# Hybrid block on one core: four subtractions of the weight split move from GpSimd to VectorE

## The chip, the cores and the metric

The kernel runs on one core of one Trainium2 chip. The metric is the device time of one launch in microseconds; the figure for a kernel is the median of its runs.

## The reference

One transformer-like layer on 256 tokens of width 1024, all in fp32. Cut to what matters:

```python
h = h + hybrid_mixer(rms_norm(h, norm_mix), w_in, conv..., gates..., norm_lru_out, norm_attn_out, w_out)
h = h + memory_cross_attention(rms_norm(h, norm_cross), mem, norm_mem, w_xq, w_xkv, w_xo)
h = h + hier_moe(rms_norm(h, norm_ffn), router weights, w_gate_up, w_down)   # 32 experts, 2 per token
return rms_norm(h, norm_final)
```

The mixer projects the tokens to five parts of 512 columns (x_lru, g_lru, q, k, v). x_lru passes a short convolution and a gated linear recurrence and is multiplied by gelu(g_lru). q, k and v go through causal attention with 8 heads of 64. Both results are normalised and multiplied with w_out. The cross attention has 4 heads of 256 over 256 memory tokens. The mixture of experts holds 32 experts of two matrices, 6 MB each expert, all of which are read.

## The kernel before

**Two phases.** Phase A computes the mixer, the cross attention and the router, and ends at about 235 us. Phase B is a loop over eight batches of four experts, whose weights flow through a ring of on-chip units; its first loads are issued during phase A, each when the memory or the half that it needs has been used up.

**The dense weights** of phase A come as 30 halves of 128 x 2048 numbers, in the order of `STREAM` (line 57): halves 0 and 1 are x_lru, 2 and 3 q, 4 and 5 k, 6 and 7 v, 8 and 9 g_lru, 10 to 13 the memory keys (xk), 14 and 15 the first columns of w_out, and so on. TensorE multiplies in a rounded format (fp32r), so each half is split in two. ScalarE copies the raw half into the rounded high part (`split_hi`, the copy of line 899), and then another engine subtracts that from the raw half to get the low part (`split_lo`: `V.tensor_tensor(... subtract)`, line 1195, on VectorE, and line 1126 on GpSimd). TensorE forms three products for each chunk: activation low by weight high, activation high by weight low, and high by high (`channels`, line 561, and `tokens`, line 575). The activations are split likewise (line 1208).

**Buffers.** Raw halves land in four buffers (`landing`, m modulo 4). The load of half m is issued by SyncE once the low part of half m-4 is there (`await_split`). The two parts of a half lie in one of three slots (m modulo 3), so the high part of half m waits until TensorE has used half m-3.

**Who subtracts.** `POOL_LO = (6, 8, 10, 12)`: GpSimd makes the low parts of these four halves, VectorE those of the others. Each engine counts on its own semaphore (`w_lo`, `w_lo_pool`), and `await_split(eng, m)` waits for both counts. GpSimd also does the second part of half 0 (line 1134), powers of -0.5 for the norms (line 1120), three steps of gelu (lines 1143, 1145 and 1147) and sums of squares (lines 1157 and 1159).

**Order.** Every engine runs a list of work written out by hand, strictly in order. Around the change VectorE does: the low parts of the memory activations (`turned_lo("Tm")`, line 1208), half 7, the rotary embedding (lines 1290 to 1295), a step of the input gate (line 1300), half 9, two steps of the recurrence's input (lines 1304 and 1305), two copies of transposed q and k, half 11, the scan (line 1310), scores and maxima (lines 1315 to 1330), half 13, two normalisations of the softmax (line 1336), half 14, a copy, the end of gelu (lines 1346 and 1347), and the low part of the recurrence's result (`ylru_lo`, line 1352), for which TensorE waits ahead of half 14. TensorE does, from half 6 on: v (halves 6 and 7), transposes of q and k, g_lru (halves 8 and 9), scores (line 618), xk (halves 10 to 13), transposes of the softmax (lines 647 to 653), half 14 and the value products.

Of the kernel before, what the change touches and what calls it, by code (L numbers as in the profile page):

```python
# [17 lines left out]
F32 = mybir.dt.float32  # L18
F32R = mybir.dt.float32r
I32 = mybir.dt.int32  # L20
ALU = mybir.AluOpType
# [46 lines left out]
            "out1", "out5", "out3", "out7", None, "xv1", "xq0", "xq1", "xq2", "xq3", None, "xv3",  # L68
            None, "xo1", None, "xo3"]

POOL_LO = (6, 8, 10, 12)


PARAMS = {}
# [126 lines left out]
def block_kernel(nc, x, mem, dense, w_gate_up, w_down, norm_final, early, late, out):  # L201
    with ExitStack() as ctx:
# [3 lines left out]
        def sem(name):  # L206
            return ctx.enter_context(nc.semaphore(name))
# [42 lines left out]
        def const(name):  # L250
            a, n = CONSTS[name]
            return ctab[:, a:a + n]

        def param(name, c=None):
            a, n = PARAMS[name][0] + N_CONSTS, PARAMS[name][1]
            return ctab[:, a:a + n] if c is None else ctab[:, a + c:a + c + 1]
# [4 lines left out]
        def pb(job):  # L261
            return bank(BANK_OF[job])
# [41 lines left out]
        def pair(src, off, c):  # L304
            return tuple(src[:, off + HALF * part:off + HALF * part + HALF].rearrange("p (c t) -> p c t", c=c)
                         for part in range(2))

        def slot(m, c):
            return pair(split_w, UNIT * (m % SLOTS_W), c)
# [6 lines left out]
        def raw(m, c):  # L316

            return landing[:, HALF * (m % RAW):HALF * (m % RAW) + HALF].rearrange("p (c t) -> p c t", c=c)

        def chunks_of(m):  # L320
            return KC if STREAM[m // 2] in BY_COLUMNS else CT


        def rt(n, m=EXPERTS):
            return small[:, 256 + 64 * n:256 + 64 * n + NH * m].rearrange("p (h e) -> p h e", h=NH)
# [13 lines left out]
        freed = [sem(f"freed{b}") for b in range(BANKS)]  # L339
        raw_loaded = [sem(f"raw_loaded{r}") for r in range(RAW)]  # L340

        w_hi, w_lo, w_lo_pool = sem("w_hi"), sem("w_lo"), sem("w_lo_pool")
        w_lo_first = sem("w_lo_first")
        half_used = sem("half_used")
        x_loaded = [sem(f"x_loaded{h}") for h in range(NH)]
# [63 lines left out]
        def await_fill(eng, job):  # L409
            eng.wait_ge(filled[BANK_OF[job]], FILLS[job])  # L410

        def await_read(eng, job):
            eng.wait_ge(freed[BANK_OF[job]], FREED_AFTER[job])

        def await_first_read(eng, job):
            eng.wait_ge(freed[BANK_OF[job]], FREED_BEFORE[job] + 1)

        def await_split(eng, m):

            by_pool = sum(n in POOL_LO for n in range(m + 1))  # L420
            eng.wait_ge(w_lo, m + 1 - by_pool)
            if by_pool:
                eng.wait_ge(w_lo_pool, by_pool)

        def await_half_used(eng, m):
            if LAST_JOB[m]:
# [7 lines left out]
        def _(sp):  # L434
# [14 lines left out]
            def load_half(m):  # L449
                if m >= RAW:  # L450
                    await_split(sp, m - RAW)
                sp.dma_start(raw(m, chunks_of(m)), half_source(m)).then_inc(raw_loaded[m % RAW], 16)
# [20 lines left out]


            await_split(sp, HALVES - 4)
            load_expert(2, 2, 0, (0,))
            await_fill(sp, "xs3")
# [4 lines left out]
            await_fill(sp, "xv3")  # L482
            load_expert(1, 1, 1)
            await_split(sp, HALVES - 3)
            load_expert(2, 2, 0, (1,))
            await_fill(sp, "xpv3")
# [627 lines left out]
        @block.gpsimd  # L1114
        def _(pool):
            nc.gpsimd.memset(xlp[:, :, 0:CONV - 1], 0.0).then_inc(zeroed, 1)
            pool.wait_ge(early_loaded, 16)

            def power(col, n, done):
                nc.gpsimd.tensor_tensor(stat[:, RS + col:RS + col + n], stat[:, MS + col:MS + col + n],  # L1120
                                        const("power")[:, 0:n], ALU.pow).then_inc(done, 1)

            def split_lo(m):
                pool.wait_ge(w_hi, m + 1)
                hi, lo = slot(m, chunks_of(m))
                nc.gpsimd.tensor_tensor(lo, raw(m, chunks_of(m)), hi.bitcast(F32), ALU.subtract).then_inc(w_lo_pool, 1)

            for stage in (1, 2):
                pool.wait_ge(meansq, stage)
                power(2 * (stage - 1), 2, rstd)  # L1130
                if stage == 1:
                    pool.wait_ge(w_hi, 1)
                    hi, lo = slot(0, KC)
                    nc.gpsimd.tensor_tensor(lo[:, CT:], raw(0, KC)[:, CT:], hi[:, CT:].bitcast(F32), ALU.subtract
                                            ).then_inc(w_lo_first, 1)
            split_lo(6)
            split_lo(8)
            split_lo(10)

            pool.wait_ge(root_ready, 1)  # L1140
            for c in range(2):
                await_read(pool, f"gl{c}")
            nc.gpsimd.tensor_tensor(gate_r, gx, gx, ALU.mult).then_inc(pool_step, 1)
            pool.wait_ge(pool_step, 1)
            nc.gpsimd.tensor_scalar(gate_r, gate_r, GELU_CUBE, 1.0, ALU.mult, ALU.add).then_inc(pool_step, 1)
            pool.wait_ge(pool_step, 2)
            nc.gpsimd.tensor_tensor(gate_r, gate_r, gx, ALU.mult).then_inc(gelu_arg, 1)
            split_lo(12)

            for part in range(2):  # L1150
                if part:
                    for c in range(2):
                        await_first_read(pool, f"pv{c}")
                else:
                    pool.wait_ge(ylru_squared, 1)
                t = CT * part
                nc.gpsimd.tensor_tensor(sqT[:, t:t + 2], sqT[:, t:t + 2], sqT[:, t + 2:t + 4], ALU.add).then_inc(pool_step, 1)
                pool.wait_ge(pool_step, 3 + part)
                nc.gpsimd.tensor_tensor(sqT[:, t], sqT[:, t], sqT[:, t + 1], ALU.add).then_inc(squares_added, 1)
            await_read(pool, "ss")  # L1160
            power(SUB, 4, sub_rstd)
            for stage in (3, 4):
                pool.wait_ge(meansq, stage)
                power(2 * (stage - 1), 2, rstd)

            pool.wait_ge(rank_known, 1)
            over = rt(12)
            nc.gpsimd.tensor_scalar(over, rankm, float(SLOTS), None, ALU.is_ge).then_inc(over_ready, 1)
            for h in range(NH):
                pool.wait_ge(final_ms, h + 1)  # L1170
                power(FINAL + h, 1, final_rstd)

        @block.vector
        def _(dve):
# [3 lines left out]
            def link(ins):  # L1178

                steps[0] += 1  # L1180
                ins.then_inc(dve_step, 1)
                dve.wait_ge(dve_step, steps[0])

            def release(ins, job):
                ins.then_inc(freed[BANK_OF[job]], 1)
# [5 lines left out]
            def split_lo(m):  # L1191

                dve.wait_ge(w_hi, m + 1)
                hi, lo = slot(m, chunks_of(m))
                V.tensor_tensor(lo, raw(m, chunks_of(m)), hi.bitcast(F32), ALU.subtract).then_inc(w_lo, 1)  # L1195
# [10 lines left out]
            def rest(dst, src, gain, hi):  # L1206

                return V.scalar_tensor_tensor(dst, src, gain, hi.bitcast(F32), ALU.mult, ALU.subtract)  # L1208

            def turned_lo(prefix, dst, gain, cs=range(4)):  # L1210
                for c in cs:
                    await_first_read(dve, f"{prefix}{c}")
                    for k in range(2):
                        t = 2 * c + k
                        i = rest(dst[1][:, t], pb(f"{prefix}{c}")[:, 256 * k:256 * k + 256], param(gain, t), dst[0][:, t])
                    release(i, f"{prefix}{c}")

            def plain(job, dst, c=2):

                await_fill(dve, job)  # L1220
                src = pb(job).rearrange("p (c t) -> p c t", c=c) if c else pb(job)
                release(V.tensor_copy(dst, src), job)
# [5 lines left out]
            hi, lo = slot(0, KC)  # L1228
# [47 lines left out]
            i.then_inc(conv_done, 1)  # L1276
            split_lo(5)
            turned_lo("Tm", ms_, "norm_mem")
            split_lo(7)

            for name in ("q", "k"):
# [16 lines left out]
            for c in range(2):  # L1298
                await_read(dve, f"ig{c}")
            link(V.scalar_tensor_tensor(gate_i, gate_i, 1.0, xc, ALU.add, ALU.mult))  # L1300
            split_lo(9)
            dve.wait_ge(decay_ready, 1)
            dve.wait_ge(root_ready, 1)
# [1 line left out]
            link(V.tensor_tensor(root, root, gate_i, ALU.mult))  # L1305
            for c in (1, 3):
                plain(f"Tqk{c}", qkT[:, 2 * c:2 * c + 2])
            split_lo(11)
            for t in range(CT):
                i = V.tensor_tensor_scan(xc[:, t], decay[:, t], root[:, t], 0.0, ALU.mult, ALU.add)  # L1310
# [17 lines left out]
            for c in range(4):  # L1328
                await_read(dve, f"s1{c}")
            V.tensor_reduce(soft[:, 8:16], p1, AX.X, ALU.max, negate=True).then_inc(smax, 1)  # L1330
            split_lo(13)

            def normalize(h, p):
# [209 lines left out]
            with dve.Fori(0, BATCHES) as g:  # L1543
# [13 lines left out]
                for j in range(BATCH):  # L1557
                    n = BATCH * g + (j + 1)
# [18 lines left out]
            with dve.If(many > 0):  # L1577
# [13 lines left out]
                with dve.Fori(0, EXPERTS) as e:  # L1591
                    for h in range(NH):
                        n = NH * e + (h + 1)
# [13 lines left out]
            for h in range(NH):  # L1607
# [3 lines left out]
                for cb in range(2):  # L1611
                    n = slice(512 * cb, 512 * cb + 512)
# [21 lines left out]
```

## Time and profile before

| what | us |
|---|---|
| median of 3 runs | 672.67 (672.4 to 674.99) |
| the profiled execution, its own time | 671.75 |
| its span | 670.0 |
| TensorE matmul busy | 510.9 (76%) |
| VectorE busy | 220.9 (33%), 425 instructions |
| ScalarE busy | 168.9 (25%) |
| GpSimd busy | 41.0 (6%), 25 instructions |
| load of a dense half, issue to landing | 5.4 (median of 30) |
| HBM traffic | 237.85 MB, mean 355 GB/s |

A line number names the line of the program that issued an instruction, which may be a helper. Times of rows are counted from the start of the span.

### The profile page before, as it was taken

The page shows a single profiled execution, that of the slowest core. Times are in us where ns is not written, and L with a number is a line of the kernel's source. Part 1 is how long each engine was busy: PE and PEld are TensorE (multiplying, and loading weights), DVE is VectorE, ACT ScalarE, POOL GpSimd, SP SyncE. Part 2 cuts the span into 40 slices and gives each one's busy share as a digit, 9 for nine tenths or more (in the row PEclk, how much of TensorE's full clock was granted, in tenths as well). Part 3 has the DMA queues.
Part 4 walks back from the last instruction along what each step waited for, and adds up shares of the span by engine and source line. Part 5 has one row for each costly group of instructions (what it writes and reads, how often), then busy time and mean ns, then how long its engine had stood idle before and what let it go on. Part 6 is the DMA issues. An engine that isn't in the chain of part 4 may idle for free.

```text
span 670.0 us, 11410 instructions
## 1 busy us (share of the span) xinstructions
PE 510.9 (76%) x4768; PEld 351.9 (53%) x4768; DVE 220.9 (33%) x425; ACT 168.9 (25%) x325; POOL 41.0 (6%) x25
## 2 busy tenths in 40 slices
PE   3999999999999987978656756855684585657544
PEld 3988998789888654545223423422352252224221
DVE  3795987664653432212011200201120021012002
ACT  6558576363441211111010100101010001011002
POOL 2032441300000000000000000000000000000000
PEclk9999999999999799999867978978698898889889
DMA  8754733396579969999999999999999999999993
GB/s 345 285 194 183 314 127 142 138 398 248 186 282 382 357 238 425 425 430 427 427 426 427 422 425 426 429 427 426 427 426 424 423 429 427 427 426 427 423 425 156
DMA packets 25637, 237.85 MB, mean 355 GB/s; under 512 B 2832, under 2 KB 2960, under 8 KB 4368
## 3 DMA queue, kind: packets, MB, share of 16 engines
q1 hardware_dynamic: 25616, 237.55, 86.0%
q8 instruction: 15, 0.25, 0.1%
q14 instruction: 6, 0.05, 0.0%
HBM read 236.49 MB, written 1.05 MB: 355 GB/s over the span
## 4 chain that ended last, share of the span: by engine, by line
SPq 48%; PE 38%; DMA 7%; issue 3%; DVE 2%; ACT 1%; POOL 1%; DVEq 0%; POOLq 0%
SPq L447 30%; SPq L442 18%; PE psum L575 14%; PE psum L561 11%; DMA ring<-in_w_down 5%; PE psum L811 3%; PE psum L836 2%; DMA landing<-in_dense 1%; PE psum L794 1%; PE psum L544 1%; PE psum L709 1%; PE psum L732 1%; PE psum L845 1%; PE psum L758 1%; POOL stat L1120 1%
## 5 line engine op out<-in xcount | busy, mean ns | idle before, releaser
L811 PE MATMUL psum<-ring,xg 128*32 128x256 f32 x2048 | 152.6, 454 | 87.4 <-DMA ring<-in_w_gate_up 87.4
L811 PEld LDWEIGHTS psum<-ring,xg 128*32 128x32 f32 x2048 | 78.8, 126 | 154.6 <-issue 129.7
L575 PE MATMUL psum<-split_w,split_act 128*128 128x512 f32 x432 | 101.8, 393 | 1.2 <-DVE res L1379 1.2
L575 PEld LDWEIGHTS psum<-split_w,split_act 128*128 128x128 f32 x432 | 80.4, 188 | 18.3 <-DVE res L1379 1.7
L1562 DVE SCALAR_TENSOR_TENSOR small<-small,psum 128x128 f32<-128x128 f32 x32 | 9.2, 288 | 214.8 <-ACT small L1084 214.8
L1084 ACT ACTIVATE small<-psum 128x128 f32<-128x128 f32 x32 | 8.9, 277 | 279.3 <-PE psum L811 279.3
L836 PE MATMUL psum<-ring,small 128*32 128x256 f32 x1024 | 67.2, 400 | 12.9 <-ACT small L899 11.7
L561 PE MATMUL psum<-split_act,split_w 128*128 128x256 f32 x576 | 72.2, 289 | 0.9 <-DVE split_act L1208 0.9
L561 PEld LDWEIGHTS psum<-split_act,split_w 128*128 128x128 f32 x576 | 71.6, 197 | 1.7 <-DVE split_w L1229 1.2
L899 ACT ACTIVATE split_w<-landing 128x2048 fp32r<-128x2048 f32 x30 | 57.4, 1915 | 51.2 <-PE psum L575 27.6
L1195 DVE TENSOR_TENSOR split_w<-landing,split_w 128x2048 fp32r<-128x2048 f32 x25 | 58.9, 2361 | 30.6 <-ACT split_w L899 30.6
L1568 DVE COPY ybuf<-psum 32x256 f32<-32x256 f32 x64 | 27.2, 424 | 95.3 <-PE psum L836 94.8
L836 PEld LDWEIGHTS psum<-ring,small 128*32 128x32 f32 x1024 | 30.2, 113 | 40.0 <-ACT small L899 18.1
L899 ACT ACTIVATE ybuf<-psum 32x256 f32<-32x256 f32 x64 | 23.9, 373 | 72.5 <-PE psum L836 72.2
L1120 POOL TENSOR_TENSOR stat<-stat,ctab 128x2 f32<-128x2 f32 (+2 forms) x7 | 6.9, 991 | 546.6 <-DVE stat L1188 536.6
L845 PE MATMUL psum<-ybuf,small 128*128 128x512 f32 x64 | 29.4, 602 | 8.6 <-DVE ybuf L1568 8.6
L828 PE MATMUL psum<-ctab,small 128*128 128x128 f32 x32 | 10.8, 338 | 30.2 <-DVE small L1564 30.2
L794 PEld LDWEIGHTS psum<-ntake,res 128*128 128x128 f32 x256 | 29.8, 192 | 3.3 <-issue 3.3
L794 PE MATMUL psum<-ntake,res 128*128 128x128 f32 x256 | 29.9, 275 | 0.0
L828 PEld LDWEIGHTS psum<-ctab,small 128*128 128x128 f32 x32 | 4.5, 141 | 47.1 <-DVE small L1564 47.1
L1552 DVE TENSOR_TENSOR xg<-psum,ctab 128x512 f32<-128x512 f32 x16 | 11.1, 691 | 44.5 <-PE psum L794 44.5
L845 PEld LDWEIGHTS psum<-ybuf,small 128*128 128x128 f32 x64 | 11.5, 189 | 23.7 <-ACT ybuf L899 12.3
(169 smaller groups left out, 348.6 us busy)
## 6 DMA issues: line engine op xcount, KB each, us to landing
ring<-in_w_gate_up SPq DMA_DIRECT2D x56, 2048.0 KB, 39.7
ring<-in_w_down SPq DMA_DIRECT2D x64, 1024.0 KB, 36.0
landing<-in_dense SPq DMA_DIRECT2D x30, 1024.0 KB, 5.4
ring<-in_w_gate_up SPq DMA_DIRECT2D x16, 1024.0 KB, 7.7
res<-in_x SPq DMA_DIRECT2D x2, 512.0 KB, 3.6
work<-in_mem SPq DMA_DIRECT2D x1, 1024.0 KB, 12.1
out<-ring SPq DMA_DIRECT2D x4, 256.0 KB, 2.0
ybuf<-in_late SPq DMA_DIRECT2D x1, 512.0 KB, 14.8
```

What stands on the lines that cost most here:

```text
L442: sp.dma_start(unit(u)[:, n], src).then_inc(loaded[u][side], 16)
L447: sp.dma_start(unit(u), w_gate_up[e, part]).then_inc(loaded[u][1], 16)
L561: i = mm(b[:, 256 * c:256 * c + 256], w[a][:, k, P * c:P * c + P], src[t][:, k, :], start=k == 0 and n == 0, stop=k == KC - 1 and n == 2)
L575: i = mm(b, src[t][:, k0 + k, P * h:P * h + P], w[a][:, k, :], start=first and k == 0 and n == 0, stop=last and k == CT - 1 and n == 2)
L794: i = mm(bank(GATHER + part)[:, P * k:P * k + P], res[:, h, P * c:P * c + P], ntake[:, h], start=h == 0, stop=h == NH - 1)
L811: i = mm(half[SLOTS * strip:SLOTS * strip + SLOTS], xg[:, CT * part + k, SLOTS * j:SLOTS * j + SLOTS], w[:, k, :, P * strip:P * strip + P] ...
L828: tr(bank(HY)[:, 256:256 + P], hid, ident).then_inc(hid_turned, 1)
L836: i = mm(bank(HY)[SLOTS * strip:SLOTS * strip + SLOTS, 0:256], hidT[:, SLOTS * k:SLOTS * k + SLOTS], w[:, k, 256 * strip:256 * strip + 256 ...
L845: i = mm(bank(ACC_BANKS[2 * h + cb]), give[:, P * h:P * h + P], ybuf[:, 512 * cb:512 * cb + 512], start=False, stop=True, skip_group_check ...
L899: return nc.scalar.activation(dst, src, ACT.Identity, scale=scale, bias=bias)
L1195: V.tensor_tensor(lo, raw(m, chunks_of(m)), hi.bitcast(F32), ALU.subtract).then_inc(w_lo, 1)
L1568: i = V.tensor_copy(ybuf[SLOTS * j:SLOTS * j + SLOTS, 256 * strip:256 * strip + 256], bank(6)[r, 0:256])
```

## The change

GpSimd no longer subtracts whole halves. VectorE makes the low parts of halves 6, 8, 10 and 12 itself, each directly ahead of the next odd half in its list, and one semaphore counts all halves.

```diff
-POOL_LO = (6, 8, 10, 12)
...
         def await_split(eng, m):
-            by_pool = sum(n in POOL_LO for n in range(m + 1))
-            eng.wait_ge(w_lo, m + 1 - by_pool)
-            if by_pool:
-                eng.wait_ge(w_lo_pool, by_pool)
+            eng.wait_ge(w_lo, m + 1)
...
-            def split_lo(m):
-                pool.wait_ge(w_hi, m + 1)
-                hi, lo = slot(m, chunks_of(m))
-                nc.gpsimd.tensor_tensor(lo, raw(m, chunks_of(m)), hi.bitcast(F32), ALU.subtract).then_inc(w_lo_pool, 1)
...
-            split_lo(6)
-            split_lo(8)
-            split_lo(10)
             pool.wait_ge(root_ready, 1)
...
             nc.gpsimd.tensor_tensor(gate_r, gate_r, gx, ALU.mult).then_inc(gelu_arg, 1)
-            split_lo(12)
...
             turned_lo("Tm", ms_, "norm_mem")
+            split_lo(6)
             split_lo(7)
...
             link(V.scalar_tensor_tensor(gate_i, gate_i, 1.0, xc, ALU.add, ALU.mult))
+            split_lo(8)
             split_lo(9)
...
                 plain(f"Tqk{c}", qkT[:, 2 * c:2 * c + 2])
+            split_lo(10)
             split_lo(11)
...
             V.tensor_reduce(soft[:, 8:16], p1, AX.X, ALU.max, negate=True).then_inc(smax, 1)
+            split_lo(12)
             split_lo(13)
```

## Rows read from the trace of the kernel before

**Rows 1.** Busy time by stretch; per engine busy us, then clock, DMA share, GB/s.
```profile
66.00:112.00 46.00, 46.00 (x379) 44.61 (x378) 41.55 (x36) 30.53 (x57) 17.75 (x7) 1.00 0.48 183
286.00:622.00 336.00, 221.12 (x2548) 117.73 (x2548) 50.72 (x144) 33.40 (x102) 0.00 (x0) 0.87 1.01 426
```
**Rows 2.** The chain that ended last, in order: start us, us, what.
```profile
82.24 23.22 PE psum L561 x192
...
107.21 0.87 PE psum L653 x8
108.08 5.60 PE psum L575 x24
...
136.40 5.47 PE psum L575 x24
...
148.22 23.03 PE psum L561 x192
```
**Rows 3.** All waits of TensorE between 25 and 135 us: total, times, longest.
```profile
PE psum L575 <- DVE res L1379: 1.2, 1, 1.2
```
**Rows 4.** TensorE in order of time: start us, us, line, operation.
```profile
54.90 11.26 PE L575 MATMUL psum<-split_w,split_act 128*128 128x512 f32 x48
...
67.66 11.76 PE L561 MATMUL psum<-split_act,split_w 128*128 128x256 f32 x96
```
**Rows 5.** GpSimd in order of time.
```profile
43.00 5.49 POOL L1126 TENSOR_TENSOR split_w<-landing,split_w 128x2048 fp32r<-128x2048 f32 x1 [18.53 <-ACT split_w L899]
53.88 4.59 POOL L1126 TENSOR_TENSOR split_w<-landing,split_w 128x2048 fp32r<-128x2048 f32 x1 [5.39 <-ACT split_w L899]
68.25 5.51 POOL L1126 TENSOR_TENSOR split_w<-landing,split_w 128x2048 fp32r<-128x2048 f32 x1 [9.79 <-ACT split_w L899]
82.08 1.90 POOL L1143 TENSOR_TENSOR work<-work 128x1024 f32<-128x1024 f32 x1 [8.32 <-ACT work L899]
...
87.56 4.64 POOL L1126 TENSOR_TENSOR split_w<-landing,split_w 128x2048 fp32r<-128x2048 f32 x1
```
**Rows 6.** VectorE in order of time.
```profile
43.91 3.22 DVE L1208 SCALAR_TENSOR_TENSOR split_act<-psum,ctab,split_act 128x256 fp32r<-128x256 f32 x8
...
54.90 3.71 DVE L1290 TENSOR_TENSOR work<-work,ctab 128x128 f32<-128x128 f32 x1 [4.21 <-ACT work L899]
...
59.67 0.28 DVE L1290 TENSOR_TENSOR work<-work,ctab 128x128 f32<-128x128 f32 x1
...
61.00 1.22 DVE L1300 SCALAR_TENSOR_TENSOR work<-work 128x1024 f32<-128x1024 f32 x1
65.86 2.29 DVE L1195 TENSOR_TENSOR split_w<-landing,split_w 128x2048 fp32r<-128x2048 f32 x1 [3.64 <-ACT split_w L899]
...
69.33 5.53 DVE L1305 TENSOR_TENSOR work<-work 128x1024 f32<-128x1024 f32 x1
...
76.09 2.28 DVE L1195 TENSOR_TENSOR split_w<-landing,split_w 128x2048 fp32r<-128x2048 f32 x1
...
90.23 4.11 DVE L1195 TENSOR_TENSOR split_w<-landing,split_w 128x2048 fp32r<-128x2048 f32 x1 [2.19 <-ACT split_w L899]
...
98.07 2.28 DVE L1195 TENSOR_TENSOR split_w<-landing,split_w 128x2048 fp32r<-128x2048 f32 x1
...
105.20 2.70 DVE L1208 SCALAR_TENSOR_TENSOR split_act<-work,ctab,split_act 128x256 fp32r<-128x256 f32 x4 [1.85 <-ACT split_act L899]
```
**Rows 7.** ScalarE in order of time.
```profile
73.76 1.92 ACT L899 ACTIVATE split_w<-landing 128x2048 fp32r<-128x2048 f32 x1 [3.65 <-PE psum L561]
...
79.52 1.91 ACT L899 ACTIVATE split_w<-landing 128x2048 fp32r<-128x2048 f32 x1 [3.35 <-PE psum L561]
...
94.04 1.04 ACT L1005 ACTIVATE work<-work 128x1024 f32<-128x1024 f32 x1
...
95.47 1.90 ACT L899 ACTIVATE split_w<-landing 128x2048 fp32r<-128x2048 f32 x1
```
**Rows 8.** Costliest groups: xcount | busy, mean ns | idle before, releaser.
```profile
L1195 DVE TENSOR_TENSOR split_w<-landing,split_w 128x2048 fp32r<-128x2048 f32 x25 | 58.9, 2361 | 30.6 <-ACT split_w L899 30.6
```

More of the change, by code:

```diff
@@ L340, in block_kernel @@
         raw_loaded = [sem(f"raw_loaded{r}") for r in range(RAW)]
-        w_hi, w_lo, w_lo_pool = sem("w_hi"), sem("w_lo"), sem("w_lo_pool")
+        w_hi, w_lo = sem("w_hi"), sem("w_lo")
         w_lo_first = sem("w_lo_first")
```

## The prediction

> **What bounds the kernel now.** I read the busy times by stretch first, then the chain that ended last, the waits of TensorE, and last the four engines in order of time. From 286 to 622 us the DMA engines are full (share 1.01, 426 GB/s) and GpSimd does nothing [rows 1]. The subtractions lie between 43 and 92 us, in phase A. There the chain is TensorE's own work, piece after piece [rows 2]: it is busy 46.00 of 46.00 us between 66 and 112 us, at the full clock [rows 1]. Its only wait between 25 and 135 us is 1.2 us ahead of line 575 [rows 3], at 126 us, for a result that no subtraction of halves 6 to 12 touches. So the change can cost time only if a low part, or something queued behind it on VectorE, comes later than TensorE asks, and it can gain only what TensorE waits for now, which is nothing that the waits show. Phase B's loads are released by TensorE's steps, so I let a delay of TensorE in phase A reach the end in full.
>
> **What goes and what comes.** GpSimd loses four instructions of 5.49, 4.59, 5.51 and 4.64 us [rows 5], 20.2 us together. VectorE gains four at the price of its own of that shape: 25 take 58.9 us [rows 8], and without the one long of 4.11 [rows 6] that is 54.8 / 24 = 2.28 us each, so 4 x 2.28 = 9.1 us.
>
> VectorE also gets time back. Three of its instructions are far longer than their shape, and each overlaps a GpSimd subtraction and ends soon after it. The first rotary product takes 3.71 us where its twin takes 0.28; it starts at 54.90 and ends at 58.61, the GpSimd one at 58.47. The product of line 1305 takes 5.53 us (1.22 for the 128x1024 of line 1300), and ends at 74.86, GpSimd's at 73.76, which is 1.10 us earlier, as long as a product of that size needs. Half 13 takes 4.11 us in place of 2.28 and ends at 94.34, GpSimd's at 92.20 [rows 5, 6]. I read this as VectorE standing still until GpSimd is done: 3.43 + 4.31 + 1.83 = 9.6 us come back. The eight activation parts of line 1208 beside GpSimd's first subtraction take 3.22 / 8 = 0.40 us each, and show no such stop [rows 6]. So VectorE's busy total hardly moves: 220.9 + 9.1 - 9.6 = 220.4 us.
>
> The Trainium skill, "SBUF — State Buffer", section "Who interferes with whom", says that a VectorE instruction with two SBUF inputs and a GpSimd instruction that reads SBUF take turns on a shared port, whoever is first for its whole length. The three long rows agree with it, and so do the eight parts of line 1208, whose one input is in PSUM. By that rule the 9.6 us return; without it they would stay, which is the first rival below. "Perfetto Trace Analysis", section "Optimizing Scalar/DVE Operations", speaks for GpSimd's help when VectorE is full, and adds that between these two it might not help. VectorE is busy 41.55 of the 46 us between 66 and 112 us [rows 1], so its idle 4.45 us take the two subtractions that move into this stretch (4.56) but for 0.1 us even with nothing returned; where they fall outside that idle time is the first rival's matter.
>
> **Step by step.** Each time is what I expect after, with the moment at which TensorE needs it. TensorE takes halves 6 and 7 at 54.9 and 60.5 us, 8 and 9 at 67.7 and 73.6 [rows 4], and 10 to 13 at 82.2, 88.0, 93.8 and 99.6 (23.22 / 4 = 5.8 us each, [rows 2]).
>
> - Half 6: VectorE ends the memory activations at 47.1 [rows 6], so 47.1 to 49.4 (GpSimd had it at 48.5); needed at 54.9. Half 7 behind it, to 51.6 (before 50.7); needed at 60.5.
> - The rotary steps wait for ScalarE until 54.9 as before and then end 3.4 us earlier, at 57.7 (before 61.1); TensorE wants them at 66.1, when v is done [rows 4]. Line 1300 follows, to 58.9.
> - Half 8: 58.9 to 61.1 (before 58.5); needed at 67.7. Half 9 waits for its high part until 65.86, as before.
> - Line 1305 ends at 70.6 in place of 74.9, the two copies at 71.8. Half 10: 71.8 to 74.1 (before 73.8); needed at 82.2.
> - Half 11 waits for ScalarE's high part, which ends at 73.76 + 1.92 = 75.7 [rows 7]: 75.7 to 77.9 (before 78.4). Scan, scores and maxima follow 0.1 to 0.4 us earlier than now, the last maximum ending at 87.7 to 88.0 (before 90.23 - 2.19 = 88.04, [rows 6]).
> - Half 12: it falls into the idle 2.19 us ahead of half 13 [rows 6] and ends at about 90.1 (before 92.2); needed at 93.8. Half 13 waits for its high part until 90.2, then takes 2.28: 92.5 (before 94.3); needed at 99.6.
> - The first normalisation ends at 93.8. The second needs ScalarE's last exponential, just ahead of the 94.04 of [rows 7], and ends at 96.7 (before 98.1). Half 14 then waits for its high part, 95.47 + 1.90 = 97.4 [rows 7], and begins 0.67 us earlier than its 98.07 of now [rows 6].
> - From there all is a chain of VectorE and ScalarE, so `ylru_lo` comes 0.67 us earlier: 107.90 [rows 6] becomes 107.2. TensorE starts half 14 at 108.08, directly behind its transposes [rows 2]. This is the tightest spot: 0.18 us to spare now, 0.85 after.
>
> No wait in the new order stands for something late. The high parts are all made before VectorE reaches them: GpSimd began on 6, 8 and 10 at 43.0, 53.9 and 68.2 [rows 5], and that of 12 ends at 79.52 + 1.91 = 81.4 [rows 7]. Behind SyncE's waits the loads of halves 10 and 12 go out 0.9 and 2.6 us later, at 49.4 and 61.1, land some 5.4 us later, and stay clear of the high parts, which ScalarE makes just ahead of 68.2 [rows 5] and at 79.5 us [rows 7]; those of 14, 16 and 17 move by +0.3, -2.1 and -1.8 us, and no engine waits for them. Gelu on GpSimd still starts at 82.1, when ScalarE has copied its input [rows 5], and is not brought forward by an empty GpSimd. The one wait fewer in `await_split` I cost at nothing, since TensorE shows no gap there.
>
> **Sum.** TensorE's path: 0 from the removal, 0 from the addition. From the profiled execution's own 671.75 us I get 671.7; the median of the runs lies 0.9 us above that execution, so I say 672.6 us. Least: TensorE may hold small waits that are too short to be listed. The block of 192 matmuls at 82 us takes 23.22 us against 23.03 for its like at 148 us, and half 14 takes 5.60 against 5.47 [rows 2]: at most 0.3 us, to 672.3. Most, with the 9.6 us not returned: 2.0 us, worked out next.
>
> **Rivals.**
> 1. *The long instructions are not GpSimd's doing and stay long.* Against it: three ends that follow GpSimd's. For it: only that three cases are few. Then line 1305 still ends at 74.9, half 10 goes to 78.4 and pushes all behind it by 2.28 us less the little that half 11's wait gives, say 2.2: maxima end at 90.25, half 12 at 92.45 (needed 93.8), half 13, with its 4.11, at 96.56 instead of 94.34. The chain to `ylru_lo` has no other gap, so it comes at 110.1, and TensorE waits 110.1 - 108.1 = 2.0 us at half 14. That gives 672.6 + 2.0 = 674.6 us, slower than before, at the one place where VectorE has least to spare. It decides as soon as VectorE comes more than 0.18 us later to the normalisations than now.
> 2. *Worse, each added subtraction also takes the longest time seen on VectorE, 4.11 us.* Halves 8, 10 and 12 then add some 0.5 + 1.8 + 1.8 us to that chain: 2.0 + 4.1 = 6.1 us, 678.8 us. Against it: 24 of VectorE's 25 average 2.28 [rows 8], and with GpSimd empty no partner is left for the 25th.
> 3. *TensorE gains what the listed waits don't show, and more.* If the contention also held up TensorE's feeding, its matmuls would be slower beside GpSimd. But halves 8 and 9, beside one subtraction, take 11.76 us, hardly more than half of the 23.22 [rows 2, 4]. A gain above 0.5% (3.4 us) needs a stall that no row shows; it would give 669 us or less.
>
> **Chances.** Forecast (change under 0.5 us) 80%, rival 1 8%, rival 2 2%, rival 3 4%, and 6% for a cause I have not named, such as another phase of the expert stream: 4% of it within 0.5%, 2% slower. About 0.5%, or 3.4 us, is what a measurement can tell from no change. Rival 1 lies within it. So: same 0.80 + 0.08 + 0.04 = 0.92, faster 0.04, slower 0.02 + 0.02 = 0.04. The range takes in rival 1 and the spread of the runs shown: 671.0 to 674.9 us.
>
> **What would show it.** GpSimd busy about 20.8 us with 21 instructions; VectorE 429 instructions and busy within 1 us of 220.4; all whole subtractions on VectorE at about 2.29 us; the first rotary product 0.28 and line 1305 1.22 us; `ylru_lo` near 107.2 us, TensorE without a wait in 25 to 125 us, half 14 at 108.1. A TensorE wait ahead of half 14 or 12, or a long row on VectorE with GpSimd idle, would make me wrong.

## The result and the profile after

The changed kernel takes 670.27 us (median of 20 runs, 667.03 to 673.07) against 674.53 us before (20 runs, 669.50 to 678.54): ratio 0.9939, 95% interval 0.992 to 0.9958. It is faster by 0.6%, where I forecast no change. The median of before in this comparison lies 1.9 us above that of its first three runs, and its runs spread over 9 us, those of after over 6.

What I said of the engines holds. The page of after, busy us, share and instructions of each engine:

```profile
PE 514.8 (77%) x4768; PEld 351.0 (52%) x4768; DVE 220.9 (33%) x429; ACT 169.1 (25%) x325; POOL 20.8 (3%) x21
```

VectorE is as busy as before (forecast 220.4 us). In order of time, start, duration, line, operation, these rows of after answer to [rows 6]:

```profile
44.06 3.23 DVE L1194 SCALAR_TENSOR_TENSOR split_act<-psum,ctab,split_act 128x256 fp32r<-128x256 f32 x8
47.19 4.49 DVE L1181 TENSOR_TENSOR split_w<-landing,split_w 128x2048 fp32r<-128x2048 f32 x2
53.05 0.29 DVE L1277 TENSOR_TENSOR work<-work,ctab 128x128 f32<-128x128 f32 x1 [1.37 <-ACT work L895]
...
67.42 1.23 DVE L1293 TENSOR_TENSOR work<-work 128x1024 f32<-128x1024 f32 x1
...
86.03 4.64 DVE L1181 TENSOR_TENSOR split_w<-landing,split_w 128x2048 fp32r<-128x2048 f32 x2
...
102.69 2.69 DVE L1194 SCALAR_TENSOR_TENSOR split_act<-work,ctab,split_act 128x256 fp32r<-128x256 f32 x4 [1.85 <-ACT split_act L895]
```

Halves 6 and 7 stand in one row of two subtractions, and so do 12 and 13. The three long rows are short: 0.29, 1.23, and 4.64 us for two halves where one took 4.11. `ylru_lo` is there at 102.69 + 2.69 = 105.38 us. TensorE in order of time, answering to [rows 4]:

```profile
14.46 11.88 PE L557 MATMUL psum<-split_act,split_w 128*128 128x256 f32 x96 [0.86 <-DVE split_act L1194]
26.18 1.91 PE L540 MATMUL psum<-ctab,work 128*128 128x128 f32 x16
27.85 22.10 PE L571 MATMUL psum<-split_w,split_act 128*128 128x512 f32 x96
49.78 3.61 PE L600 MATMUL psum<-work,ybuf 128*128 128x256 f32 x16
53.05 11.26 PE L571 MATMUL psum<-split_w,split_act 128*128 128x512 f32 x48
```

From 53 us on the order and the durations are those of before, 1.85 us earlier. On the chain half 14 starts at 106.23, so `ylru_lo` has 0.85 us to spare, as forecast. All 1.85 us were won in the first row, the 96 matmuls of x_lru, which no part of the change touches (2.05 us shorter, less a start 0.16 us later). In the profiled execution of before it looked like this (same view):

```profile
14.30 13.93 PE L561 MATMUL psum<-split_act,split_w 128*128 128x256 f32 x96 [0.88 <-DVE split_act L1208]
```

The two profiled executions have spans of 670.0 and 669.3 us, while the medians lie 4.3 us apart. So the gain could not be read from this pair. I ran the kernel before again.

### The profile page after: what moved, and what is told of

Read it like the earlier page. It is cut to its first block, busy times and chain, and to the rows that moved or that the text cites. A ratio compares the mean times of both kernels' runs of the same rounds, so it can differ in the third digit from the quotient of the medians.

```text
span 669.3 us, 11375 instructions
## 1 busy us (share of the span) xinstructions
PE 514.8 (77%) x4768; PEld 351.0 (52%) x4768; DVE 220.9 (33%) x429; ACT 169.1 (25%) x325; POOL 20.8 (3%) x21
## 4 chain that ended last, share of the span: by engine, by line
SPq 46%; PE 39%; DMA 8%; issue 3%; DVE 2%; ACT 1%; POOL 1%; DVEq 0%; POOLq 0%
SPq L443 29%; SPq L438 17%; PE psum L571 14%; PE psum L557 10%; DMA ring<-in_w_gate_up 7%; PE psum L807 4%; PE psum L832 2%; DMA landing<-in_dense 1%; PE psum L790 1%; PE psum L540 1%; PE psum L728 1%; PE psum L705 1%; PE psum L841 1%; PE psum L754 1%; POOL stat L1116 1%
## 5 line engine op out<-in xcount | busy, mean ns | idle before, releaser
L807 PE MATMUL psum<-ring,xg 128*32 128x256 f32 x2048 | 157.1, 464 | 81.2 <-DMA ring<-in_w_gate_up 81.2
L832 PE MATMUL psum<-ring,small 128*32 128x256 f32 x1024 | 68.6, 407 | 12.8 <-ACT small L895 11.7
L1181 DVE TENSOR_TENSOR split_w<-landing,split_w 128x2048 fp32r<-128x2048 f32 x29 | 66.2, 2289 | 30.9 <-ACT split_w L895 30.8
L557 PE MATMUL psum<-split_act,split_w 128*128 128x256 f32 x576 | 70.1, 284 | 0.9 <-DVE split_act L1194 0.9
L557 PEld LDWEIGHTS psum<-split_act,split_w 128*128 128x128 f32 x576 | 69.5, 192 | 1.6 <-DVE split_w L1215 1.2
L841 PE MATMUL psum<-ybuf,small 128*128 128x512 f32 x64 | 31.3, 635 | 8.6 <-DVE ybuf L1558 8.6
```

The source lines that it names most:

```text
L557: i = mm(b[:, 256 * c:256 * c + 256], w[a][:, k, P * c:P * c + P], src[t][:, k, :], start=k == 0 and n == 0, stop=k == KC - 1 and n == 2)
L807: i = mm(half[SLOTS * strip:SLOTS * strip + SLOTS], xg[:, CT * part + k, SLOTS * j:SLOTS * j + SLOTS], w[:, k, :, P * strip:P * strip + P] ...
L832: i = mm(bank(HY)[SLOTS * strip:SLOTS * strip + SLOTS, 0:256], hidT[:, SLOTS * k:SLOTS * k + SLOTS], w[:, k, 256 * strip:256 * strip + 256 ...
L841: i = mm(bank(ACC_BANKS[2 * h + cb]), give[:, P * h:P * h + P], ybuf[:, 512 * cb:512 * cb + 512], start=False, stop=True, skip_group_check ...
```

## The experiments

Each was compared with fresh runs of the kernel before on the same chip; before's medians there were 674.82, 674.54 and 673.85 us.

**The kernel before, unchanged (null).**

> The kernel before, unchanged in its work, as a control. Theory C (chance and the state of the chip explain the 0.6%): its times spread as widely as those of before (669.5 to 678.5 us) and its ratio to before is 1.000 within 0.003. Theory G (GpSimd's subtractions cost something in most executions that the one profiled execution did not show): ratio 1.000 too. A ratio off 1.000 by over 0.003 would mean that the comparison itself is worth less than its interval. The profile gives a second look at the first 30 us, where x_lru took 13.93 us before and 11.88 after.

Measured: 677.67 us (12 runs, 672.68 to 680.76), ratio 1.0034 (1.0002 to 1.0067). The interval just leaves out 1, so these comparisons are worth some 0.3% less than they say. The 35 runs of before beside it suggest why: 12 lie between 669.4 and 672.9 us, 13 between 676.7 and 678.9, and 10 in the nearly 4 us between. They lie in two loose groups, near 672 and near 678 us, and a median over few runs depends on how many fall in each. The profiled execution of this run, 677.86 us, is of the upper group, that of before, 671.75, of the lower. VectorE, ScalarE and GpSimd in the upper one, each in order of time:

```profile
34.99 1.38 DVE L1271 TENSOR_SCALAR work<-work,ctab 128x256 f32<-128x256 f32 x4
36.41 9.46 DVE L1273 SCALAR_TENSOR_TENSOR work<-work,ctab 128x256 f32<-128x256 f32 x12
45.79 2.28 DVE L1195 TENSOR_TENSOR split_w<-landing,split_w 128x2048 fp32r<-128x2048 f32 x1
...
38.61 1.92 ACT L899 ACTIVATE split_w<-landing 128x2048 fp32r<-128x2048 f32 x1 [0.60 <-PE psum L575]
...
40.61 4.58 POOL L1126 TENSOR_TENSOR split_w<-landing,split_w 128x2048 fp32r<-128x2048 f32 x1 [16.43 <-ACT split_w L899]
```

and TensorE there:

```profile
14.00 11.87 PE L561 MATMUL psum<-split_act,split_w 128*128 128x256 f32 x96 [1.00 <-DVE split_act L1208]
25.71 1.91 PE L544 MATMUL psum<-ctab,work 128*128 128x128 f32 x16
27.37 16.58 PE L575 MATMUL psum<-split_w,split_act 128*128 128x512 f32 x72
48.12 8.34 PE L575 MATMUL psum<-split_w,split_act 128*128 128x512 f32 x24 [4.17 <-DVE split_w L1195]
```

The same rows in the lower group, from the profile of before:

```profile
36.71 5.09 DVE L1273 SCALAR_TENSOR_TENSOR work<-work,ctab 128x256 f32<-128x256 f32 x12
41.71 2.29 DVE L1195 TENSOR_TENSOR split_w<-landing,split_w 128x2048 fp32r<-128x2048 f32 x1
...
41.01 1.92 ACT L899 ACTIVATE split_w<-landing 128x2048 fp32r<-128x2048 f32 x1 [0.61 <-PE psum L575]
```

Read the two sets side by side. x_lru takes 11.87 us in one and 13.93 in the other, so TensorE frees the slot for half 6 earlier, ScalarE makes its high part at 38.61 in place of 41.01, and GpSimd starts at 40.61 in place of 43.00 [rows 5]. VectorE's convolution would end at about 41.5 either way. In the lower group GpSimd comes 1.3 us after it, finds VectorE in half 5 and pays itself (5.49 us for 4.6). In the upper group it comes 0.9 us before the end: the 12 taps, whose two inputs both lie in SBUF, take 9.46 us in place of 5.09, and end at 45.87, just after GpSimd's end at 45.19. Half 5 comes at 48.07, and TensorE, which wanted it at 43.95, waits 4.17 us. Busy time by stretch then shows what the wait costs besides (busy us of TensorE, its loads, VectorE, ScalarE, GpSimd, then the granted clock, DMA share, GB/s):

```profile
44.00:46.00 2.00, 0.00 (x0) 0.00 (x0) 2.00 (x3) 1.91 (x1) 1.19 (x1) 1.00 0.00 0
46.00:48.00 2.00, 0.00 (x0) 0.00 (x0) 2.00 (x2) 0.00 (x0) 0.00 (x0) 0.72 0.00 0
48.00:50.00 2.00, 1.88 (x5) 1.49 (x6) 2.00 (x7) 0.00 (x0) 0.00 (x0) 0.50 0.42 78
50.00:52.00 2.00, 2.00 (x6) 1.61 (x5) 2.00 (x5) 0.00 (x0) 0.00 (x0) 0.50 0.96 393
52.00:54.00 2.00, 2.00 (x6) 1.54 (x6) 1.40 (x1) 0.00 (x0) 0.00 (x0) 0.57 1.03 434
54.00:56.00 2.00, 2.00 (x10) 1.66 (x9) 0.00 (x0) 0.00 (x0) 0.00 (x0) 1.00 0.93 348
```

TensorE had stood idle, and its granted clock then is 0.50, which is the lower level of 1.2 GHz: it does 5 or 6 matmuls in 2 us where it does 10 at a granted clock of 1.00. Half 5 takes 8.34 us in place of 5.47. Together 4.17 + 2.87 = 7.0 us, and the spans of null and after, both with x_lru at 11.9 us, differ by 676.1 - 669.3 = 6.8 us. At the start of the second block of 192 matmuls (148.22 in [rows 2]), which stands at 152.89 us in null and at 146.22 in after, 6.67 us of it are already there.

This gave theory R: the gain is the end of one race at half 6. Its rivals were C, chance, and S (called G2 in the expectations of pool12 and pool6810), a price for each subtraction on GpSimd.

**The changed kernel again (after2).**

> The changed kernel once more. Theory G: ratio about 0.994 again (670.3 against 674.5 us) with the narrower spread. Theory C: ratio between 0.997 and 1.003.

Measured: 670.76 us (668.39 to 674.58), ratio 0.9954 (0.992 to 0.9987). The gain repeats. The upper end of this interval still lies in C's range, but 1 lies outside it and outside the interval of the first 20 runs, and the unchanged kernel beside it came out at 1.0034; so C falls.

**Half 12 alone stays on GpSimd (pool12), and half 12 alone moves (pool6810).**

```diff
-POOL_LO = (6, 8, 10, 12)
+POOL_LO = (12, )        # pool12; (6, 8, 10, ) in pool6810
```

> GpSimd subtracts only half 12; halves 6, 8 and 10 are VectorE's. Theory G1 (the loss sits in the handing over of half 12 and its lock on the way to ylru_lo, where TensorE has 0.18 us to spare): ratio 1.000, nothing is gained. Theory G2 (each GpSimd subtraction costs about the same, about 1 us): ratio 0.9955, a gain of 3 us. Theory C: 1.000. In the profile half 13 still takes over 4 us on VectorE and the product of line 1305 1.2 us.

> The counterpart: only half 12 goes to VectorE. Theory G1: ratio 0.994, the whole gain. Theory G2: 0.9985, a gain of 1 us. Theory C: 1.000. In the profile half 13 takes 2.28 us and ylru_lo has 0.8 us to spare.

Measured: pool12 671.47 us, ratio 0.9941 (0.9912 to 0.9971); pool6810 674.94 us, ratio 0.9997 (0.9963 to 1.0031). Both are the opposite of G1, my own first idea that the tightest spot, `ylru_lo`, was to blame. Half 12 costs nothing that these runs can tell, and the loss lies in 6, 8 and 10. G2 is not out yet: its 0.9955 and 0.9985 lie inside the two intervals. The profiled execution of pool6810 was one of those with x_lru at 11.88 us, and all waits of TensorE between 25 and 135 us there are:

```profile
PE psum L575 <- DVE split_w L1194: 4.2, 1, 4.2
PE psum L575 <- DVE res L1379: 1.2, 1, 1.2
```

**Half 6 alone on GpSimd (pool6), and half 6 alone moved (pool81012).** The same edit with `(6, )` and `(8, 10, 12, )`.

> GpSimd subtracts half 6 alone. Theory R (race for half 6: where TensorE's first matmuls get the full clock early, GpSimd begins half 6 inside VectorE's last convolution tap, VectorE stands still, half 5 comes 4.4 us late, TensorE waits 4.2 us and then works some 7 us at the lower clock): all of the loss stays, ratio 0.998 to 1.004 to before, times in two groups near 671 and 677 us. Theory S (a price for every subtraction on GpSimd): a quarter of it, ratio about 0.9955.

> GpSimd subtracts halves 8, 10 and 12, VectorE half 6. Theory R: the loss is gone, ratio 0.992 to 0.996, one group at 669 to 673 us, though VectorE still stands 3.4, 4.3 and 1.8 us in the profile. Theory S: three quarters of the loss stay, ratio about 0.9985.

Measured: pool6 675.83 us, ratio 1.0022 (0.9986 to 1.0058), with runs from 670.68 to 680.64 and none between 674.4 and 677.3; pool81012 670.76 us, ratio 0.9934 (0.9905 to 0.9962). Half 6 carries the loss, and the other three nothing that these runs can tell. S falls: pool6's interval leaves out the 0.9955 it expected, and pool81012's its 0.9985. The profile of pool81012 still has the three long rows on VectorE, at 3.71, 5.54 and 4.11 us; so the 9.6 us of VectorE's time, which the change gives back, are not the gain. In pool6's profiled execution x_lru took 13.74 us and TensorE lost nothing; again GpSimd came inside half 5, and was the one to wait:

```profile
42.05 5.67 POOL L1126 TENSOR_TENSOR split_w<-landing,split_w 128x2048 fp32r<-128x2048 f32 x1 [18.34 <-ACT split_w L899]
```

**GpSimd keeps all four, but starts half 6 after half 5 (held6).**

```diff
+            pool.wait_ge(w_lo, 6)
             split_lo(6)
```

> The kernel before, all four subtractions still on GpSimd, but it begins half 6 only when VectorE has finished half 5. Theory R (only the race at half 6 costs): the upper group is gone and the whole gain is there, ratio 0.992 to 0.996, though GpSimd does as much as before. Theory S (work on GpSimd costs): ratio 1.000. In the profile half 6 starts at 42 to 44 us on GpSimd, the convolution's 12 taps take 5.1 us, TensorE has no wait in 25 to 100 us.

Measured: 671.68 us, ratio 0.9951 (0.992 to 0.9981). One wait more gives the gain with not one subtraction moved, and S, with its 1.000, is out here too. Its profile has x_lru at 11.88 us, the case that used to lose; GpSimd, then VectorE, in order of time:

```profile
43.69 4.63 POOL L1126 TENSOR_TENSOR split_w<-landing,split_w 128x2048 fp32r<-128x2048 f32 x1 [19.58 <-DVE split_w L1196]
...
36.32 5.09 DVE L1274 SCALAR_TENSOR_TENSOR work<-work,ctab 128x256 f32<-128x256 f32 x12
41.33 2.28 DVE L1196 TENSOR_TENSOR split_w<-landing,split_w 128x2048 fp32r<-128x2048 f32 x1
43.53 3.22 DVE L1209 SCALAR_TENSOR_TENSOR split_act<-psum,ctab,split_act 128x256 fp32r<-128x256 f32 x8
46.67 3.80 DVE L1196 TENSOR_TENSOR split_w<-landing,split_w 128x2048 fp32r<-128x2048 f32 x1
```

Half 7 now waits for GpSimd (3.80 us), where it has time; TensorE's only wait up to 135 us is the 1.2 us of [rows 3].

**Extra matmuls at the start, in the kernel before and in the changed one (warm_before, warm_after).** They are on a zeroed tile, into a bank that is not in use yet.

```diff
+            pe.wait_ge(warm_ready, 1)
+            for k in range(36):
+                mm(bank(7)[:, 0:128], hidT, hidT, start=True, stop=True)
             pe.wait_ge(early_loaded, 16)
```

> The kernel before with 36 extra matmuls on a zeroed tile ahead of TensorE's first work, in its idle first 9 us; their results are used by nothing. If they give the full clock at 14 us in every execution, theory R expects all executions in the upper group, median 677 to 678 us, ratio 1.003 to 1.006: an earlier TensorE makes the kernel slower. Theory U (the start of TensorE has nothing to do with the two groups): two groups, ratio 1.000, or 0.998 from the 2 us won at the start.

> The same extra matmuls in the changed kernel. Theory R: no race is left to lose, so the start is only won, up to 2 us in the executions that had the low clock there: 668 to 670.5 us, ratio 0.990 to 0.994, a narrow spread. Theory U: as the changed kernel, 0.994 or 0.995 with its spread.

Measured: warm_before 676.07 us, ratio 1.0031 (1.0 to 1.0061), none of its 12 runs under 673.65, where before beside it has 16 of 35; warm_after 670.79 us, ratio 0.995 (0.9916 to 0.9983), with runs from 667.82 to 675.08. The ratio of warm_before alone doesn't exclude U, whose 1.000 is the edge of its interval; that the lower group is missing does. So an earlier TensorE makes the kernel before slower and not the changed one, as R says. Two of R's figures were missed: the median of 676.1 is 1 to 2 us too low, and warm_after shows neither the gain at the start nor the narrow spread (its 0.995 is what U said). What stands behind either is not shown. In warm_before's profiled execution the race is lost and the wait is 4.28 us; the profile lists each of the 36 extra matmuls as two:

```profile
1.05 10.87 PE L589 MATMUL psum<-small 128*128 128x128 f32 x72 [1.05 <-DVE small L1228]
11.76 1.91 PE L545 MATMUL psum<-ctab,work 128*128 128x128 f32 x16
14.43 11.87 PE L562 MATMUL psum<-split_act,split_w 128*128 128x256 f32 x96 [0.76 <-DVE split_act L1212]
...
48.84 8.26 PE L576 MATMUL psum<-split_w,split_act 128*128 128x512 f32 x24 [4.28 <-DVE split_w L1199]
```

The extra work runs to 11.9 us and holds up the first transposes (11.76; 9.78 before), so I tried fewer.

**26 extra matmuls, in the changed kernel and in held6 (warm26_after, warm26_held6).**

> The changed kernel with 26 in place of 36 extra matmuls, so that they end by 9 us and delay no transpose. Expected: x_lru in 11.9 us in every execution; 668 to 670.5 us, ratio 0.991 to 0.994 to before, at most 1 us under the changed kernel.

> Both: GpSimd keeps its four subtractions with half 6 held back, and TensorE is warmed by 26 extra matmuls. Theory R: the same 668 to 670.5 us as with the changed kernel warmed, ratio 0.991 to 0.994, where the kernel before warmed gave 676.1 us. Theory S: 674 us or more.

Measured: 671.30 us, ratio 0.995 (0.992 to 0.9981), and 670.10 us, ratio 0.9931 (0.9904 to 0.9958). The first misses its figure: x_lru took 13.11 us in its profiled execution, so 26 matmuls don't always give the quick start, and no gain over the changed kernel can be measured. The second agrees with R and excludes S, whose 674 us or more is a ratio of 1.000 here. None of after, pool81012, held6 and the warmed ones can be told from the others; nothing beats the changed kernel beyond its interval.

**What else moves the times.** The race is not all that spreads them. From the start of the second block of 192 matmuls to the end of the span no edit moves any work, and still this part takes between 519.9 us (the two with 36 extra matmuls) and 526.7 us (pool12) in the thirteen profiled executions. pool12's profiled execution took 675.67 us and warm26_held6's 674.79, well above the lower group, and neither had the wait ahead of half 5. In both the granted clock was low near the end. Here is a late stretch of before, with its last four matmuls on the chain, and then the same of pool12:

```profile
656.00:662.00 6.00, 4.42 (x38) 1.89 (x38) 1.23 (x4) 1.12 (x4) 0.00 (x0) 1.00 0.16 63
...
659.91 1.97 PE psum L845 x4
```

```profile
656.00:662.00 6.00, 4.19 (x34) 1.67 (x34) 1.32 (x4) 1.02 (x3) 0.00 (x0) 0.50 0.03 12
...
661.93 3.77 PE psum L845 x4
```

So a long time alone is no sign of a lost race; the wait ahead of half 5 in a profile is. This spread also blurs the two groups: of the first 20 runs of before, 8 lie between 672.9 and 676.7 us. What decides where the clock falls late in the kernel stays open.

## Why the prediction was wrong

**Right.** GpSimd's busy time and instructions, VectorE's (220.9 us for 220.4), the 9.6 us that come back and the 9.1 that are added, the starts around the four subtractions (those that wait for TensorE once its 1.85 us are allowed for), 0.85 us to spare at `ylru_lo`, and no cost from the addition that any run shows. Rivals 1 and 2 are out: with GpSimd empty no long row is left on VectorE. pool12 and pool6810 show that the tightest spot of the profile never mattered.

**The step that failed** is in the first part: the change "can gain only what TensorE waits for now, which is nothing that the waits show". It took one execution for all. That execution had x_lru at 13.93 us and was of the lower group. Of the nine profiled executions without extra matmuls, five have x_lru at 11.87 or 11.88 us, four at 13.7 to 13.9. Of those kernels that let GpSimd start half 6 freely, before and pool6 had the slow start and no wait, null and pool6810 the quick start and the 4.2 us wait; warm_before too. So I estimate that the kernel before loses 7.0 us in a bit over half of its executions and nothing in the rest: 7.0 x 5/9 = 3.9 us, near the 4.3 us between the medians. Nine executions are few for such a share, and of the rest only two, before and pool6, were seen. The level of the forecast, 672.6 us, was off besides: it added the 0.9 us by which the median of three runs lay above the profiled execution, and over 20 runs this is 2.8 us.

**It was in the rows.** Under "What goes and what comes" I looked for GpSimd's subtractions that overlap a long row, found three, and of the first asked only what it does to the activation parts behind half 5. At 43.00 [rows 5] it started only 1.3 us after VectorE had left the convolution, whose 12 taps take 5.09 us and read twice from SBUF. Its start hangs on TensorE (`[18.53 <-ACT split_w L899]`, and ScalarE in turn on TensorE), that of the convolution on VectorE's own list, on which it has no idle time from 30 us up to there. Two chains with no order between them, a shared resource and 1.3 us of distance: that is a race, and its price could have been worked out with the very durations that I used: half 5 some 4.4 us late, where even this slow-started TensorE wanted it 2.3 us after it was made, which leaves a wait of some 2 us. Half 5 was not in my list of steps because the change doesn't name it.

Rival 3 asked for a stall that no row shows and got 4%. Its form was wrong (I put it down to slower matmuls). Its size was right as a gain, above 3.4 us with 4.3 measured; its level of 669 us or less was not reached, as the median of before had risen by 1.9 us.

The Trainium skill, "SBUF — State Buffer", section "Who interferes with whom", adds that issue order decides which of the two is blocked. The two groups are the two orders: GpSimd 5.49 us behind VectorE, VectorE's taps 9.46 us behind GpSimd. I had used the rule for what the change gives back, and not for what the order might be in another execution.

## What to carry to other kernels

Where two engines share a resource, list not only the overlaps of one profile but also the near misses, and ask of each whether one chain of semaphores sets both starts; if not, price the other order. Look at all the times of a kernel before trusting its profile: two groups of runs can mean that the profile shows only one of two courses that the program takes, and here a second profile, from the other group, told more than a closer look at the first. The cheap cure is a wait that fixes the order (held6). Moving the work cures it too, as far as these runs tell for no other reason.

## What was not expected of the hardware

An idle stretch of 4.2 us on TensorE cost 2.9 us more behind it: the granted clock was 0.72 in its last 2 us, then 0.50 for the next 4 us and more, and 1.00 at 54 us.

The start of TensorE differs between executions of the same program: 96 matmuls in 11.9 or in 13.7 to 13.9 us. From 15 to 18 us it does 26 matmuls in after and 16 in before, at a granted clock that reads 1.00 in both:

```profile
15.00:18.00 3.00, 3.00 (x26) 2.98 (x25) 2.64 (x6) 1.99 (x2) 0.77 (x1) 1.00 1.02 421
```

```profile
15.00:18.00 3.00, 3.00 (x16) 3.00 (x15) 2.65 (x5) 1.82 (x2) 0.60 (x1) 1.00 1.02 421
```

36 matmuls ahead gave the quick start in both profiled executions, 26 in one of two. In the other (warm26_after, 13.11 us) TensorE had waited 2.33 us ahead of x_lru, and there the record does show the lower level, with nearly the pace of before:

```profile
14.00:17.00 3.00, 3.00 (x14) 3.00 (x15) 2.65 (x7) 2.44 (x3) 1.21 (x1) 0.50 0.99 414
```

In warm26_held6 it had waited 2.53 us at the same place, the granted clock stayed at 1.00, and x_lru took 11.88 us. So the slow start looks like a start at the lower level that the record of before doesn't show. That is not proved, and what decides it stays open.
